# Two layers of an encoder on one core: turns at the head, a halved last tile, a second engine for the last output tile

## What is computed

```python
def swiglu(h, w_gate, w_up, w_down):
    return (jax.nn.silu(h @ w_gate) * (h @ w_up)) @ w_down
...
for i in range(DEPTH):      # DEPTH = 2
    x = x + 0.5 * swiglu(rmsnorm(x, norm_ff1[i]), ff1_w_gate[i], ff1_w_up[i], ff1_w_down[i])
    x = x + token_mixer(rmsnorm(x, norm_mix[i]), w_in[i], ...)
    x = x + 0.5 * swiglu(rmsnorm(x, norm_ff2[i]), ff2_w_gate[i], ff2_w_up[i], ff2_w_down[i])
    g = jax.nn.sigmoid(rmsnorm(x, norm_ple[i]) @ ple_w_gate[i])
    x = x + g * (p[i] @ ple_w_proj[i])
return rmsnorm(x, norm_final)
```

## Time and profile before

| | us |
|---|---|
| median of 3 executions | 1184.9 (1184.19 to 1185.09) |
| the profiled execution | 1185.89 |
| span of the profiled execution | 1183.2 |
| TensorE busy | 1172.2 (99%) |
| VectorE busy | 814.6 (69%) |
| ScalarE busy | 593.5 (50%) |
| GpSimd busy | 121.5 (10%) |
| bytes moved | 218.86 MB, 185 GB/s |

### The profile page before, as it was taken

The page is one execution under the profiler, slowest core; times in us unless marked ns, Lnnn a source line. Parts: engine busy times, 40 slices in busy tenths (PEclk is TensorE's granted clock), DMA queues, the critical chain, the costliest instruction groups (busy, mean ns, idle before and its releaser), DMA issues.

```text
span 1183.2 us, 23927 instructions
## 1 busy us (share of the span) xinstructions
PE 1172.2 (99%) x10470; PEld 1146.8 (97%) x10470; DVE 814.6 (69%) x939; ACT 593.5 (50%) x669; POOL 121.5 (10%) x136
## 2 busy tenths in 40 slices
PE   9999999999999999999999999999999999999997
PEld 8999999999999999999999999999899999999996
DVE  5866555688978766655786665558798777666455
ACT  5544435555745544444554444456466455444443
POOL 2000001012511000001210000100033020000011
PEclk9999999999999999999999999999999999999998
DMA  7655555545445556555555555554635365555541
GB/s 287 234 204 186 196 196 181 179 165 192 143 144 200 202 182 209 181 202 189 179 199 197 194 198 186 200 203 135 212 136 176 111 224 211 180 203 189 184 173 36
DMA packets 33383, 218.86 MB, mean 185 GB/s; under 512 B 5184, under 2 KB 6016, under 8 KB 7296
## 3 DMA queue, kind: packets, MB, share of 16 engines
q1 hardware_dynamic: 33280, 217.34, 53.1%
HBM read 216.15 MB, written 1.05 MB: 184 GB/s over the span
## 4 chain that ended last, share of the span: by engine, by line
PE 98%; DVE 1%; DMA 1%; ACT 0%; issue 0%; POOL 0%; SPq 0%; POOLq 0%; DVEq 0%
PE psum L381 31%; PE psum L383 31%; PE psum L382 31%; PE psum L513 1%; PE psum L647 1%; DMA x_all<-in_x 1%; PE psum L627 1%; PE psum L611 0%; PE psum L680 0%; PE psum L420 0%; PE psum L596 0%; PE psum L691 0%; DVE gates L1641 0%; PE psum L714 0%; DVE hB_lo L1616 0%
## 5 line engine op out<-in xcount | busy, mean ns | idle before, releaser
L1194 DVE TENSOR_TENSOR w_lo<-raw,w_hi 128x2048 fp32r<-128x2048 f32 x200 | 457.2, 2290 | 213.8 <-ACT w_hi L837 213.8
L837 ACT ACTIVATE w_hi<-raw 128x2048 fp32r<-128x2048 f32 x201 | 385.1, 1917 | 365.4 <-PE psum L383 358.1
L381 PE MATMUL psum<-hA_hi,w_hi 128*128 128x256 f32 x1360 | 378.1, 278 | 0.0
L382 PE MATMUL psum<-hA_hi,w_lo 128*128 128x256 f32 x1360 | 375.7, 276 | 0.0
L383 PE MATMUL psum<-hA_lo,w_hi 128*128 128x256 f32 x1360 | 375.6, 276 | 0.0
L381 PEld LDWEIGHTS psum<-hA_hi,w_hi 128*128 128x128 f32 x1360 | 255.3, 188 | 3.2 <-issue 2.7
L382 PEld LDWEIGHTS psum<-hA_hi,w_lo 128*128 128x128 f32 x1360 | 255.4, 188 | 0.0
L383 PEld LDWEIGHTS psum<-hA_lo,w_hi 128*128 128x128 f32 x1360 | 255.3, 188 | 0.0
L381 PE MATMUL psum<-hB_hi,w_hi 128*128 128x256 f32 x832 | 230.3, 277 | 1.5 <-DVE w_lo L1624 1.4
L382 PE MATMUL psum<-hB_hi,w_lo 128*128 128x256 f32 x832 | 229.7, 276 | 0.0
L383 PE MATMUL psum<-hB_lo,w_hi 128*128 128x256 f32 x832 | 229.7, 276 | 0.0
(11 more groups left out here) (178 smaller groups left out, 1227.7 us busy)
## 6 DMA issues: line engine op xcount, KB each, us to landing
raw<-in_weights SPq DMA_DIRECT2D x203, 1024.0 KB, 4.9
raw<-in_weights SPq DMA_DIRECT2D x2, 512.0 KB, 6.5
out<-gates SPq DMA_DIRECT2D x3, 256.0 KB, 2.2
x_all<-in_x SPq DMA_DIRECT2D x1, 520.0 KB, 3.9
x_all<-in_x SPq DMA_DIRECT2D x1, 512.0 KB, 6.5
relu<-in_p SPq DMA_DIRECT2D x2, 256.0 KB, 5.1
consts<-in_consts SPq DMA_DIRECT2D x1, 384.0 KB, 5.6
out<-gates SPq DMA_DIRECT2D x2, 128.0 KB, 2.3
```

What stands on the lines that cost most here:

```text
L381: pe.matmul(o, lh, rh, start=start, stop=False)
L382: pe.matmul(o, ll, rh, start=False, stop=False)
L837: act.activation(w_hi[:, s, :], raw[:, s, :], ACT.Copy).then_inc(hi_ready[s], 1)
L1194: dve.tensor_tensor(w_lo[:, s, :], raw[:, s, :], w_hi[:, s, :].bitcast(F32), ALU.subtract).then_inc(lo_ready[s], 1)
```

## The change

- **Turns at the head.** On ScalarE and VectorE, piece 2 of chunk 0 now stands behind tiles 4 and 5, piece 3 behind tiles 6 and 7. Pieces 0 and 1 stay behind tiles 0 to 3.
- **Fourth chunk.** ScalarE's `squares(0, 0, 3)` moves behind the split of chunk 3 (the fourth), into `ffn`.
- **Last tile in halves.** In layer 2, x tile 7 goes through VectorE, ScalarE and the squares in two operations of 128 tokens each; TensorE's last sums wait for each half by itself.
- **GpSimd.** TensorE spreads the factors a second time, into bank 5; ScalarE copies them to `rb`; GpSimd multiplies tile 7 of `final` by `rb`. VectorE keeps four operations (2, 2, 2, 1 tiles). SP issues tile 7's store third, behind a wait for GpSimd, ahead of the stores of tiles 4 and 5 and of tile 6. VectorE no longer waits for both of ScalarE's last two scaled tiles ahead of its first operation.

```diff
-STORES = (slice(0, 2), slice(2, 4), slice(4, 6), slice(6, 7), slice(7, 8))
+VECTOR_ENDS = (slice(0, 2), slice(2, 4), slice(4, 6), slice(6, 7))
+POOL_END = slice(7, 8)
...
@@ sync @@
-            for i, tiles in enumerate(STORES):
+            def store(tiles):
+                sp.dma_start(out[:, tiles, :], final[:, tiles, :]).then_inc(stored, 16)
+
+            for i in range(4):
                 sp.wait_ge(out_ready, i + 1)
-                sp.dma_start(out[:, tiles, :], final[:, tiles, :]).then_inc(stored, 16)
-            sp.wait_ge(stored, 16 * len(STORES))
+                store(VECTOR_ENDS[i])
+                if i == 1:
+                    sp.wait_ge(out_pool, 1)
+                    store(POOL_END)
+            sp.wait_ge(stored, 16 * 5)
@@ tensor @@
                 if L == L_N:
                     pe.matmul(bank[b][:, 0:T], ones[:, :], diag[:, :, :].rearrange("p a t -> p (a t)"), start=True, stop=True
                               ).then_inc(rb_sum, 1)
+                    pe.matmul(bank[5][:, 0:T], ones[:, :], diag[:, :, :].rearrange("p a t -> p (a t)"), start=True, stop=True
+                              ).then_inc(end_sum, 1)
                     return
...
             for c in range(3):
-                if c:
-                    pe.wait_ge(last_squares, c)
                 for t in range(2):
                     half = slice(t * P, (t + 1) * P)
+                    if c:
+                        pe.wait_ge(last_squares, c if c == 1 else c + t)
@@ scalar @@
                     split(L, n + 3)
+                    if n == 0 and L == 0:
+                        squares(0, 0, 3)
                     if g == 0:
                         split(L, n + 4)
...
-                for c in range(2):
+                for c in range(1 if last else 2):
...
                 if last:
+                    for t in range(2):
+                        half = slice(t * P, (t + 1) * P)
+                        act.wait_ge(end_scaled, t + 1)
+                        act.activation(gate_act[:, 1, half], gate_sum[:, 1, half], ACT.Tanh, scale=0.5).then_inc(end_tanh, 1)
+                    for t in range(2):
+                        half = slice(t * P, (t + 1) * P)
+                        act.wait_ge(end_added, t + 1)
+                        act.activation(last_squared[:, 1, half], x[:, 7, half], ACT.Square).then_inc(last_squares, 1)
...
-                act.wait_ge(landed[0] if i else half_landed, 16)
-                for m in (2 * i, 2 * i + 1):
+                    if i == 0 and m == 0:
+                        continue
+                    act.wait_ge(landed[0] if i else half_landed, 16)
+                    if i == 0:
+                        act.activation(w_hi[:, 0, piece(0)], raw[:, 0, piece(0)], ACT.Copy).then_inc(piece_hi, 1)
                     act.activation(w_hi[:, 0, piece(m)], raw[:, 0, piece(m)], ACT.Copy).then_inc(piece_hi if m < 3 else hi_ready[0], 1)
...
             squares(0, 0, 2)
-            squares(0, 0, 3)
             for L in range(L_N - 1):
                 layer(L, False)
             layer(L_N - 1, True)
+            act.wait_ge(end_sum, 1)
+            act.activation(rb[:, :], bank[5][:, 0:T], ACT.Copy).then_inc(end_spread, 1)
@@ gpsimd @@
             layer(L_N - 1, True)
+            pool.wait_ge(end_spread, 1)
+            pool.wait_ge(final_scaled, 2)
+            pool.tensor_tensor(final[:, 7, :], final[:, 7, :], rb[:, :], ALU.mult).then_inc(out_pool, 1)
@@ vector @@
                 if last:
+                    chunk_products(L, PGATE + 3)
+                    for t in range(2):
+                        half = slice(t * P, (t + 1) * P)
+                        dve.tensor_tensor(gate_sum[:, 1, half], bank[LAST_TILES[1]][:, half], rb[:, half], ALU.mult).then_inc(end_scaled, 1)
+                    for t in range(2):
+                        half = slice(t * P, (t + 1) * P)
+                        g, xs = gate_act[:, 1, half], x[:, 7, half]
+                        dve.wait_ge(end_tanh, t + 1)
+                        step(L, dve.scalar_tensor_tensor(out=g, in0=g, scalar=1.0, in1=tiles(3)[:, 1, half], op0=ALU.add, op1=ALU.mult))
+                        dve.scalar_tensor_tensor(out=xs, in0=g, scalar=0.5, in1=xs, op0=ALU.mult, op1=ALU.add).then_inc(end_added, 1)
                     mean_square(L, 4, 4)
...
-            dve.wait_ge(final_scaled, 2)
-            for m in STORES:
+            for m in VECTOR_ENDS:
                 n = m.stop - m.start
+                if n == 1:
+                    dve.wait_ge(final_scaled, 1)
                 dve.tensor_tensor(final[:, m, :], final[:, m, :], bank[4][:, 0:T].unsqueeze(1).to_broadcast([P, n, T]), ALU.mult
                                   ).then_inc(out_ready, 1)
```

More of the change, by code:

```diff
@@ L247, in hybrid_trunk @@
         tile_hi = sem("tile_hi")
+        end_scaled = sem("end_scaled")
+        end_tanh = sem("end_tanh")
+        end_added = sem("end_added")
+        end_sum = sem("end_sum")
+        end_spread = sem("end_spread")
+        out_pool = sem("out_pool")
         last_squares = sem("last_squares")
@@ L1607, in layer @@
                 embed(L, last)
-                assert steps[0] == VECTOR_STEPS, steps
+                assert steps[0] == VECTOR_STEPS + last, steps
                 steps[0] = 0
@@ L1618, in _ @@
                     ins.then_inc(h_ready, 1)
-                for m in (2 * i, 2 * i + 1):
-                    if m < 3:
-                        dve.wait_ge(piece_hi, m + 1)
-                    else:
-                        dve.wait_ge(hi_ready[0], 1)
-                    dve.tensor_tensor(w_lo[:, 0, piece(m)], raw[:, 0, piece(m)], w_hi[:, 0, piece(m)].bitcast(F32), ALU.subtract
-                                      ).then_inc(piece_lo if m < 3 else lo_ready[0], 1)
+                    if m == 0:
+                        continue
+                    for q in (0, 1) if i == 0 else (m,):
+                        if q < 3:
+                            dve.wait_ge(piece_hi, q + 1)
+                        else:
+                            dve.wait_ge(hi_ready[0], 1)
+                        dve.tensor_tensor(w_lo[:, 0, piece(q)], raw[:, 0, piece(q)], w_hi[:, 0, piece(q)].bitcast(F32), ALU.subtract
+                                          ).then_inc(piece_lo if q < 3 else lo_ready[0], 1)
             for i in range(4):
```

## The result

| | before | after |
|---|---|---|
| median of 10 executions (lowest to highest) | 1184.93 (1184.19 to 1185.70) | 1188.27 (1186.71 to 1189.77) |
| ratio with 95% interval | | 1.0029 (1.0021 to 1.0038) |
| the profiled execution, its span | 1185.89, 1183.2 | 1188.03, 1185.9 |

The change makes the kernel 3.3 us slower. That is above the predicted 1186.3 and above the upper end of the range, 1187.3. The time is nearest to the rival that got a chance of 0.05, 1187.8: the stop in the head costs TensorE its full clock.

The account below looks back on a forecast made before the run. TensorE bounds the kernel (busy 1172.2 of 1183.2 us), so only head and tail count: head +1.57, tail -0.33 + 0.16 = -0.17, together +1.4 on 1184.9, giving 1186.3 us; range 1185.7 to 1187.0, opened to 1184.7 to 1187.3.

Parts of the forecast that it names:

- Part 1: Head, turns of tiles and pieces: TensorE 0.31 earlier at 11.15, taken back at 22.49; value between 0.2 of loss and 0.
- Part 2: Head, fourth chunk's split ahead of squares: VectorE's subtraction holds GpSimd's additions, token sums at 24.06 instead of 22.49, +1.57 us.
- the case at hand was the one that the prediction gave for 17.6 to 17.7: Head, fourth chunk landing at 17.6 to 17.7: GpSimd gets in first, VectorE starts late, GpSimd's chain ends near 23.7.
- Parts 3 and 4: Tail: last x tile in halves gains 0.33; GpSimd scaling tile 8 costs 0.16 as the store queue briefly runs dry.
- rival (c): Head: the stop before the token sums costs TensorE its full clock for 2.9 us; +2.9, 1187.8 us; chance 0.05.
- the prediction's own signs of being wrong: Head: token sums (L420) starting before 23, or the granted clock showing 0.5.

Follow-up runs that it names:

- part 2 alone: Kernel before with only the last head squares moved behind the fourth chunk's split, run twice: 1186.99 us (ratio 1.0016) and 1186.30 us (1.0011).
- the seven filler products: Changed kernel plus seven unread products of ones by ones on TensorE ahead of the token sums: 1186.75 us, ratio 1.0012.
- the kernel with the longer stop: Changed kernel plus a GpSimd memset of 1024 unused columns ahead of its last two additions in the head: 1189.59 us, ratio 1.0037.

## Why the prediction was wrong

- **Part 1, as forecast.** No stop at 11.15, piece 3 in time, and the 0.31 taken back at the sums (0.35 of waiting with the squares in their old place, nothing gained from first to last product). Its value appears only when the sums move, 0.29.
- **Part 2, the stall: right in its mechanism, slightly too large.** Forecast was +1.57, with the token sums at 24.06; measured was 23.71, which is +1.22. The fourth chunk came at 17.4, 0.9 earlier than forecast, so the case at hand was the one that the prediction gave for 17.6 to 17.7: GpSimd first, VectorE late, end near 23.7 (measured 23.65). GpSimd ended 0.59 behind VectorE's subtraction, as 0.60 did in the earlier trace rows, and again 0.59 in both traces of part 2 alone. The Trainium skill (SBUF — State Buffer, "A bandwidth-pool intuition that's wrong (but worth ruling out)") gives a waiting time of about 115 ns after VectorE's end, measured there on a DMA whose descriptors GpSimd writes; with a whole addition of 0.73 behind it, it would have been an estimated 0.85 here, and the traces decide for 0.59.
- **Parts 3 and 4, as forecast.** -0.31 for -0.33 and +0.14 for +0.16. The second spread ended 0.85 behind the first (forecast 0.86); tile 8's store was issued at F + 1.35 (forecast 1.47).
- **The step that failed: rival (c).** The prediction put the price of half clock at 1.45 us beside the stall; it measured 1.6 to 1.7, since half clock lasted 3.4 us and not 2.9. The size was near, but the prediction made it hang on a condition: "It decides only if the stop comes near 2.9; 1.9 doesn't." The 2.9 was the distance in the tail between the last product and a slice seen at half clock, one case at one place. I took that distance for the shortest stop that does harm, which one case can't show, and gave 0.05. It wasn't a stop of 2.9 either. Of these 2.9 us TensorE stood still for at most 1.02 in one piece, up to the sums at 1173.08, and worked on the sums in most of the rest, as the kernel before shows (columns as in the earlier trace rows) and already the first line of the earlier trace rows with its 0.74:

```profile
1172.00:1173.00 1.00, 0.06 (x1) 0.00 (x0) 0.42 (x1) 0.50 (x2) 0.92 (x2) 1.00 0.00 0
1173.00:1174.00 1.00, 0.92 (x8) 0.92 (x8) 0.85 (x2) 0.08 (x1) 0.02 (x1) 1.00 0.00 0
```

So the tail was a case of half clock behind a shorter unbroken stop than the head's 1.9 us, and could not speak against (c). The other case I leaned on, full clock over 1.4 us ahead of the first product, is again one case. The runs showed half clock behind stops of 1.7, 1.85 and 2.3 us, and by the spans in 15 of 18 executions of this kernel. A granted clock of 0.5 in the head was also among the prediction's own signs of being wrong. With (c) as the likeliest, its sum of 1187.8 stands 0.5 below the median. What decides in which executions the clock falls stays open.
- Where there was no fall, the sum held: three executions of the changed kernel without it took 1185.89, 1185.94 and 1186.71, and the seven filler products brought 1186.75, all within 0.5 us of 1186.3.

## What to carry over

A stop of TensorE has two prices, its length and what follows at half clock; when the trace of before has one harmless and one harmful stop, the second price of anything between (and near) them has to be carried as a case of its own, at several tenths and not at 0.05. Ahead of a move that fills a hole on one engine, look at which engines that hole protected: here ScalarE's idle 3.3 us kept VectorE out of GpSimd's way. And a saving ahead of a wait without slack is worth nothing until the wait is moved, so move the consumer (here the token sums by 24 products) first.

## What the runs showed of the hardware

- Where the clock fell in the head, half clock lasted 3.4 us in each trace with a stop of 1.7 to 2.3 us, and 6.7 us behind one of 3.4. With a stop of the same length the fall cost 1.70 us from the first to the last product (1166.52 against 1164.82). It began 0.5 us after the restart, 0.6, 1.8, and once before it (in the kernel with the longer stop); so it isn't bound to a fixed distance from the stop.
- The same kernel falls to half clock behind its stop in some executions and not in others. Two traces of the changed kernel show it with stops of 1.85 and 1.87 us, once with and once without. The median depends on how often it happens: by the spans 15 of 18 in the changed kernel, 4 of 22 with part 2 alone.
- The exclusion between VectorE's subtraction (two inputs in SBUF) and GpSimd's addition works both ways: 2.86 for 2.29 when GpSimd was in first, 1.99 to 2.81 for 0.73 when VectorE was (2.81 for the addition at 19.22 in the run with seven products). In each case of the second kind in the head the addition ended 0.59 or 0.60 behind the subtraction.
- Ten unread products in the tail, where TensorE otherwise stands idle, kept the clock at 1.00 and took 0.5 us off the spread behind them.
